# A three-block network on one core: a linear fed by a layer norm's result before the next norm's root is known, re-divided work on the state-space heads, and weight slabs loaded beside the ring

## The reference

```python
# block 1, mixer, state-space part (16 heads of 64, 2 groups)
seg = exp(where(causal, a_cs[l] - a_cs[s], -inf))        # per head, 512 x 512, lower triangle
att = (C @ B.T) * seg
y   = att @ (x * dt)
...
# end of block 1 and start of block 2
x = layer_norm(ALPHA * x + conv_glu_ffn(x), ln3_g, ln3_b)
h = rms_norm(x, norm_mix_2)            # x / sqrt(mean(x^2) + eps) * norm_mix_2
proj = h @ w_in_2                      # first piece: w2_ax, then w2_ac, w2_ab, w2_rx, ...
...
# end of block 2: product-key experts, 8 heads x 16 rows of the expert table per token
q = rms_norm(x, norm_ffn_2) @ w_q_2
rows = expert_table[top16(q @ keys)]   # 512 tokens x 128 rows x 8 KB
y = sum(gelu(rows_u @ h) * gate * rows_v)
```

## Time and profile before

| | before |
|---|---|
| time, median of 3 runs | 3936.34 us (3932.47 to 3937.8) |
| the profiled execution: its own time | 3933.06 us |
| the profiled execution: its span | 3931.0 us |
| mean granted TensorE clock, share of full speed | 0.991 |
| PE busy | 3580.0 us, 91% |
| DVE busy | 2293.1 us, 58% |
| ACT busy | 1487.3 us, 38% |
| POOL busy | 1248.4 us, 32% |
| moved by DMA | 790.33 MB, 201 GB/s over the span |

### The profile page before, as it was taken

One profiled execution on the slowest core, in us unless ns is written; L12 is line 12 of the kernel. 1 busy time (PEld: TensorE's weight loads), 2 busy tenths in 40 slices (PEclk: granted clock), 3 DMA queues, 4 the chain that ended last, 5 costly groups with the idle time before them and its releaser, 6 DMA issues. The chain is left out here.

```text
span 3931.0 us, 39053 instructions
## 1 busy us (share of the span) xinstructions
PE 3580.0 (91%) x14166; PEld 2375.6 (60%) x14166; DVE 2293.1 (58%) x4220; ACT 1487.3 (38%) x3070; POOL 1248.4 (32%) x842
## 2 busy tenths in 40 slices
PE   9989998999999999999777777778779999999999
PEld 7856686788778778643232232232338667678887
DVE  4774533666746374577776777777752863364161
ACT  1233343543232453244444444445443554333222
POOL 0012352454410014233333333333332222244443
PEclk9999999999999999999999999999999999999999
DMA  3211231225622222699999999999972111122222
GB/s 125 91 58 61 68 127 52 77 97 197 256 74 98 89 88 96 268 421 421 418 409 421 421 406 422 421 401 421 421 326 96 54 60 65 57 94 87 96 97 86
DMA packets 113675, 790.33 MB, mean 201 GB/s; under 512 B 13072, under 2 KB 13264, under 8 KB 21840
## 3 DMA queue, kind: packets, MB, share of 16 engines
q0 software_dynamic: 73728, 536.90, 33.0%
q1 hardware_dynamic: 39760, 250.97, 17.9%
HBM read 785.73 MB, written 2.10 MB: 200 GB/s over the span
## 5 line engine op out<-in xcount | busy, mean ns | idle before, releaser
L3134 PE MATMUL bank<-arena 128*128 128x512 f32 x1984 | 965.3, 614 | 244.3 <-ACT arena L3189 222.8
L3134 PEld LDWEIGHTS bank<-arena 128*128 128x128 f32 x1984 | 348.9, 191 | 826.1 <-issue 805.4
L3237 DVE SCALAR_TENSOR_TENSOR arena<-arena,bank 128x1024 f32<-128x1024 f32 x512 | 624.6, 1220 | 345.6 <-DMA arena<-in_experts,arena 341.2
L999 PE MATMUL bank<-rounded,weights_hi 128*128 128x512 f32 (+1 forms) x2056 | 795.1, 387 | 24.0 <-DVE rounded L1099 7.4
L938 POOL TENSOR_TENSOR weights_lo<-weight_ring,weights_hi 128x1024 fp32r<-128x1024 f32 (+3 forms) x219 | 512.0, 2339 | 935.8 <-ACT weights_hi L1027 935.6
L1000 PE MATMUL bank<-rounded,weights_hi 128*128 128x512 f32 (+1 forms) x2056 | 791.7, 385 | 0.0
L1001 PE MATMUL bank<-rounded,weights_lo 128*128 128x512 f32 (+1 forms) x2056 | 791.6, 385 | 0.0
L3224 POOL DMA_INDIRECT arena<-in_experts,arena x512 | 481.5, 940 | 851.7 <-PE bank L3134 712.3
L1027 ACT ACTIVATE weights_hi<-weight_ring 128x1024 fp32r<-128x1024 f32 (+3 forms) x271 | 270.1, 997 | 707.9 <-PE bank L1001 705.7
L999 PEld LDWEIGHTS bank<-rounded,weights_hi 128*128 128x128 f32 x2056 | 386.9, 188 | 110.4 <-issue 22.1
L1001 PEld LDWEIGHTS bank<-rounded,weights_lo 128*128 128x128 f32 x2056 | 387.0, 188 | 77.2
(11 more groups left out here) (467 smaller groups left out, 4530.0 us busy)
## 6 DMA issues: line engine op xcount, KB each, us to landing
arena<-in_w_ada SPq DMA_DIRECT2D x48, 512.0 KB, 8.2
weight_ring<-in_w_up SPq DMA_DIRECT2D x22, 1024.0 KB
weight_ring<-in_w_down SPq DMA_DIRECT2D x8, 1408.0 KB
weight_ring<-in_w_ga SPq DMA_DIRECT2D x8, 1024.0 KB
weight_ring<-in_w_gb SPq DMA_DIRECT2D x8, 1024.0 KB
weight_ring<-in_w_q SPq DMA_DIRECT2D x8, 1024.0 KB
arena<-in_experts,arena POOLq DMA_INDIRECT x512
weight_ring<-in_w_mlp1a SPq DMA_DIRECT2D x8, 1024.0 KB
```

The lines of the kernel that those rows point to most:

```text
L999: pe.matmul(out, hi[:, k - k0, :], x.hi(k), start=first, stop=False)
L3134: mm = pe.matmul(total[:, half * T:(half + 1) * T], diag[:, j, :], rows[:, j, D + half * T:D + (half + 1) * T], start=i % SLOTS == 0, stop ...
L3237: dve.scalar_tensor_tensor(row, row, 1.0, tokens(i // SLOTS), ALU.mult, ALU.mult, accum_out=dots[:, i:i + 1]).then_inc(s.dotted.sem, 1)
```

## The change

Three places are rewritten.

1. **State-space heads.** The cumulative sums are put as two rounded parts (`acs_parts`, 48 rows, with zeros between) and spread by one rounded matmul with a chooser of two ones. DVE's differences cover only the first 128 tokens of each segment; ACT takes the exponential of the rest straight from the bank with the negated column as bias (three instructions) and of the clipped parts in two more. The weighing is divided: DVE the first segment (512), POOL the other three (768). `sums` waits for `exp_ready` of the head four before, no longer for `diff_ready`, and `heads` for POOL too.
2. **The seam.** `w2_ax` takes the layer norm's result times the next norm's weights (`WithoutRoot`: the split halves come from x * gain, without the root). Squares, their sum and the root are made while `w2_ax` runs (`RootBeside`), and `w2_ax` is taken by DVE with a multiplication by the spread inverse root (`take_scaled`). `s.n` and `s.n_split` are made during `w2_ax` for the linears behind it. Of the last group of `modulate`, 4 rows are folded ahead of the taking of the last `w_down` tile, 2 remain in `w2_ax`.
3. **Slabs.** Slabs 2, 3 and 4 of `w2_q` go to free places of the arena (`aside`) as soon as the block begins; the ring takes slabs 5, 6, 7 and those of `w3_nq`.

```diff
-        pe.matmul(self.sum_bank(h), s.eye[0:SSD_HEADS, h:h + 1].broadcast_to([SSD_HEADS, P]), self.acs, start=True, stop=True).then_inc(self.bc_ready.sem, 1)
+        pe.matmul(self.sum_bank(h), self.choose[:, h:h + 1].broadcast_to([3 * SSD_HEADS, P]), self.acs_parts, start=True, stop=True).then_inc(self.bc_ready.sem, 1)
...
     def exp(self, act, h):
+
+        att = self.att[h % 4]
         act.wait_ge(self.diff_ready.sem, self.diff_ready.at(h + 1))
-        act.activation(self.att[h % 4], self.att[h % 4], ACT.Exp).then_inc(self.exp_ready.sem, 1)
...
+        for a in range(TT - 1):
+            act.activation(att[:, SEG[a] + P:SEG[a] + seg_width(a)], self.sum_bank(h)[:, (a + 1) * P:T], ACT.Exp, bias=self.minus_acs[:, a, h:h + 1])
...
+    def weigh_first(self, dve, h):
+        self.weigh(dve, h, (0,), self.att_ready)
+
+    def weigh_others(self, pool, h):
...
+        self.weigh(pool, h, (1, 2, 3), self.others_ready)
...
+    def on_act(self, act, first_weights):
+        x, y = self.first, self.later
...
+        for k in range(DT):
+            self.high(act, k)
+            x.shift(act, k)
+            yield
...
+    def add_made(self, dve, t):
+        for k in {2: (0, 1), 3: (2, 3), 4: (4, 5), 5: (6, 7), 6: ()}.get(t, ()):
+            self.first.scale(dve, k)
+        for k in {3: (0, 1), 4: (2, 3), 5: (4, 5), 6: (6, 7)}.get(t, ()):
+            self.low(dve, k)
...
+    def sum_up(self, pe, t):
+        x = self.first
+        if t == 1:
+            pe.wait_ge(x.used.sem, x.used.at(DT - 1))
+            x.columns(pe, self.total, True, True).then_inc(x.used.sem, 1)
+
+    def midway(self, pe, t):
+        if t == 3:
+            self.first.spreads(pe)
...
+        sync.wait_ge(s.units_done.sem, unit0)
+        for j in aside:
+            sync.wait_ge(*landed(j - RING))
+            sync.dma_start(place(j), s.I["w2_q"][j]).then_inc(landed(j)[0], 16)
```

More of the change, by code:

```diff
@@ L824, in _ @@
         def _(pool):
+            other = beside.pool(pool) if beside.pool else iter(())
             for n in range(ahead, count):
@@ L828, in _ @@
                 pool.tensor_tensor(lo, raw(n), hi.bitcast(F32), ALU.subtract).then_inc(s.lo_made.sem, 1)
+                next(other, None)
             next_low(pool)
+            for _ in other:
+                pass
     if fresh:
@@ L1417, in on_dve, with __init__, high, low @@
             self.low(dve, DT - 1)
+class WithoutRoot(Seam):
+    def __init__(self, s, behind, norm, later, gain_shift, shift_ready, squares):
+        Seam.__init__(self, s, behind, norm)
+        self.later, self.gain_shift, self.shift_ready, self.squares = later, gain_shift, shift_ready, squares
+    def high(self, act, k):
+        x = self.first
+        act.wait_ge(x.scaled.sem, x.scaled.at(k + 1))
+        act.activation(self.split.hi(k), x.dst[:, k, :], ACT.Identity, bias=self.gain_shift[:, k:k + 1], scale=self.later.gain[:, k:k + 1]).then_inc(self.s.act_hi.sem, 1)
+    def low(self, dve, k):
+        x = self.first
+        dve.wait_ge(self.s.act_hi.sem, self.s.act_hi.at(self.round0 + k + 1))
+        dve.wait_ge(x.kept.sem, x.kept.at(k + 1))
+        dve.scalar_tensor_tensor(self.split.lo(k), x.dst[:, k, :], self.later.gain[:, k:k + 1], self.split.hi(k).bitcast(F32), ALU.mult, ALU.subtract).then_inc(self.s.act_lo.sem, 1)
+    def on_act(self, act, first_weights):
+        x, y = self.first, self.later
+        x.ready_for_root(act)
+        yield
+        for t in range(DT):
+            x.square(act, t, (x.centred, x.centred.at(t + 1)))
+            yield
+        x.take_root(act)
+        yield
+        first_weights()
+        act.wait_ge(self.shift_ready.sem, self.shift_ready.at(1))
+        for k in range(DT):
+            self.high(act, k)
+            x.shift(act, k)
+            yield
+        for k in range(DT):
+            act.wait_ge(x.kept.sem, x.kept.at(k + 1))
+            act.activation(self.squares[:, k, :], x.dst[:, k, :], ACT.Square).then_inc(y.squared.sem, 1)
+            yield
+    def add_squares(self, dve):
+        y, total = self.later, self.squares[:, 0, :]
+        for k in range(1, DT):
+            dve.wait_ge(y.squared.sem, y.squared.at(k + 1))
+            if k >= 2:
+                dve.wait_ge(y.used.sem, y.used.at(k - 1))
+            dve.tensor_tensor(total, total, self.squares[:, k, :], ALU.add).then_inc(y.used.sem, 1)
@@ new lines, with __init__, square_made, midway @@
+class RootBeside(Seam):
+    def __init__(self, s, behind, norm, total):
+        Seam.__init__(self, s, behind, norm)
+        self.total = total
+    def add_made(self, dve, t):
[3 more added lines that the diff above has]
+            self.low(dve, k)
+    def square_made(self, act, t):
+        if t == 2:
+            self.first.take_root(act)
+        for k in {3: (0, 1), 4: (2, 3), 5: (4, 5), 6: (6, 7)}.get(t, ()):
+            self.high(act, k)
+    def sum_up(self, pe, t):
+        x = self.first
+        if t == 1:
+            pe.wait_ge(x.used.sem, x.used.at(DT - 1))
+            x.columns(pe, self.total, True, True).then_inc(x.used.sem, 1)
+    def midway(self, pe, t):
+        if t == 3:
+            self.first.spreads(pe)
+    def on_pe(self, pe):
+        yield
+    def on_act(self, act, first_weights):
+        yield
+    def on_dve(self, dve):
+        pass
@@ L1813, in steps_on_dve, with part_rows @@
         dve.tensor_tensor_scan(self.acs, w, d, 0.0, ALU.mult, ALU.add).then_inc(s.rows_done.sem, 1)
+    def part_rows(self, dve, step):
+        s, (high, low) = self.s, (self.acs_parts[k:k + SSD_HEADS, :] for k in (0, 2 * SSD_HEADS))
+        n = 3 * SSD_HEADS
+        dve.tensor_tensor(self.choose, s.eye[0:n, 0:SSD_HEADS], s.eye[0:n, 2 * SSD_HEADS:n], ALU.add)
+        dve.wait_ge(s.rows_done.sem, s.rows_done.at(1))
+        step(dve.tensor_copy(high, self.acs))
+        dve.tensor_tensor(low, self.acs, high.bitcast(F32), ALU.subtract).then_inc(self.cols_ready.sem, 1)
     def turn_rows(self, pe):
```

116 lines of the change are left out of this document (85 added, 31 removed).

## The result

The changed kernel takes 3908.84 us (median of 4 executions, 3907.36 to 3913.55), the kernel before 3937.07 beside it (3932.47 to 3941.18). The ratio is 0.9936, with a 95% interval of 0.9923 to 0.995: faster by 0.5 to 0.8%, where 3906 and 0.8% were predicted. The changed kernel again, later and in five executions, gave 3911.59 against 3935.38, a ratio of 0.9941 (0.9929 to 0.9954). One execution of experiment 6 took 5056 us at a granted clock of 0.761: its median of six counts it, its ratio leaves it out.

The account below looks back on a forecast made before the run. It took DVE to bound the heads, a pure chain the seam and DMA the experts; 11 + 12 + 7.5 = 30.5 us less than 3936.3 gave 3906 us, 0.8% faster, with 8 in 10 between 3896 and 3919.

Parts of the forecast that it names:

- Slabs, -7.5 forecast: Experts' start: three slabs loaded into idle DMA ahead of the first gather save 2.5 us each; from -3 to -8.
- Slabs 5 and 6 now fill just that time: Experts, 1635 to 1700: slabs still loaded while PE is always busy; if DMA runs dry, part of 7.5 us is lost.
- Seam, -12 forecast: Layer norm to `w2_ax`: first matmul 14.5 us earlier, 2.3 us added on PE inside `w2_ax`; from -8 to -13.5.
- up to 1: Ahead of the last `w_down` taking: four foldings are hidden, but two held up by POOL cost up to 1 us.
- PE still runs at its own pace: Inside `w2_ax`: an input tile costs ACT 1.38 us and PE 1.38 us, so PE is not slowed.
- the rival's waits, for `s.n` or at tile 0: Seam: DVE is late and PE waits; -6 us in place of -12, 3912 us; chance 0.12.
- Heads, -11 forecast: State-space heads: period per pair falls from 6.84 to 5.2 us, 11.5 less over seven; from 0 to -17.
- I give back 1.5: Heads: low halves between POOL's weighings and DVE's added row steps, with the first pair about 1 us earlier, cost 1.5 us.
- the products take turns: Heads: POOL's and DVE's weighings do not overlap, 2 x (1.8 + 0.65) = 4.9 us a pair.
- The rival built on it (POOL always first, 8.0 a pair): Heads: DVE's product waits out POOL's for each head, next differences behind it; +8 us on the heads, 3925 us; chance 0.07.
- PE did not pace the heads as a whole: Rival that PE, at 4.4 us a pair, bounds the heads: period near 4.5, heads -16, 3901 us; chance 0.15.
- Single file: Heads: next pair's differences wait for everything of the pair ahead, 9.8 us a pair; 3937.5 us; chance 0.03.

Follow-up runs that it names:

- experiment 6: Changed kernel with the next block's two w_nq slabs loaded only when the last gather has landed; 3910.24 us, ratio 0.9936 to the kernel before.
- experiment 5: Changed kernel with five slabs of w2_q beside the ring instead of three, slabs 5 and 6 in the empty weight halves; 3903.19 us, ratio 0.9917.
- experiment 2: Changed kernel with the whole weighing, all 1280 columns, on DVE and none on POOL; 3906.05 us, ratio 0.9927 to the kernel before.
- experiment 3: Changed kernel with segments 0 and 1 (896 columns) weighed by DVE and 384 columns by POOL; 3906.79 us, ratio 0.9928 to the kernel before.
- experiment 4: Changed kernel with POOL's weighing of each head waiting for DVE's of the same head; 3917.54 us in a single execution.

## Why the prediction was right, and where a term was off

**What bounds each place** was read rightly. Three stages, one behind the other, each with its own limit: each part taken away gives back its own stage and touches no other (of the experts' 6.7 us, 5.7).

**Slabs, -7.5 forecast, 6.7 measured** (5.9 between the gathers; the other 0.9 is not theirs, as the result shows). "Slabs 5 and 6 now fill just that time" came true. What is missing lies in part just where the prediction feared for DMA, in these windows of the changed kernel:

```profile
1640.00:1650.00 10.00, 10.00 (x27) 4.63 (x26) 8.85 (x25) 2.44 (x9) 3.76 (x4) 1.00 1.01 398
1650.00:1660.00 10.00, 10.00 (x25) 4.37 (x24) 9.24 (x26) 4.65 (x16) 4.62 (x5) 1.00 1.00 396
```

At 398 and 396 GB/s for 421, 1.1 us is lost. But DMA's share stays at 1.01 and 1.00, so these rows don't show it idle, and whether it waited for PE there stays open. The next two slabs of experiment 5 were worth their full 2.5 us each.

**Seam, -12 forecast, 9.7 measured.** Its foldings cost 0.5 us, as "up to 1" allowed: 1064.73 less the 8.39 us that the program was early at this point is 1056.34, and the tile is taken at 1056.83. The first matmul came 13.4 us ahead, not 14.5, since the first scaling was 0.75 late and the chain from it to the matmul took 3.27 and not 2.9. The column sums with their wait (0.54 + 0.91) and the spread (0.81, to the next matmul at 1097.39) make 2.26 inside `w2_ax`, the 2.3 of the sum. The step that was wrong is "PE still runs at its own pace". From the first matmul to the 49th, that is over eight input tiles, it was 1107.75 - 1096.74 = 11.01 before and is 1086.68 - 1074.96 = 11.72 now. I had set ACT's 1.38 us a tile beside PE's 1.38 and called it even; ACT's two operations with the hand-over from DVE in each second tile need 1.49. That is 0.7 us. None of the rival's waits, for `s.n` or at tile 0, came. That leaves 13.4 - 2.3 - 0.7 = 10.4 for the measured 9.7. The issues of SP place 0.3 of the rest: what the seam has won is 10.0 us at `w2_ab` (1164.69 - 8.39 - 1146.30), still 9.9 at `w2_o` and 9.65 at `w2_q`. The other 0.4 I can't place.

**Heads, -11 forecast, 8.7 measured.** The period away from disturbances was forecast at 5.2 and is 5.35, and POOL's 1.8 us for 768 columns is 1.82. The mis-sized term is "I give back 1.5" for what stands between weighings. Three of seven periods are 6.6 to 6.9, which costs (6.84 - 5.35) + (6.63 - 5.35) + (6.91 - 5.35) = 4.3 us; the first `heads` comes 1.4 us earlier in its stage, where the prediction had about 1.

- In the first and the sixth period, 3.0 us together, POOL has a low half (234.48 and 264.13). It holds up POOL's own next weighing, and in the first period DVE's product too. I counted it once.
- In the fifth, 1.3 us, the loss is ACT's: a high half of weights and a tile of `w_z`, 1.45 us in a row, push back the exponentials that both weighings wait for. The prediction priced ACT at 3.2 to 3.9 us a pair without these two, so this term stood at nothing.

How the 0.5 us by which two periods are too long in experiment 2, and the 0.9 in experiment 3, divide between ACT and POOL was not tried.

Deeper lies a mistake that the sum hid. I took "the products take turns" from the earlier trace rows and found 4.9 us a pair, but did not work out the same pair *without* POOL. With the durations of the earlier trace rows that is 2 x (1.5 + 4 x 0.34) + 0.7 = 6.4, which would have spoken for dividing. But successive instructions of DVE overlap: four differences take 1.04 from start to start and not 1.37, a product 1.40 and not 1.50, so it is 5.5. The gain of dividing was thus 0.2 us a pair and not 1.2, too little to pay for the long periods.

The rule of the Trainium skill that the prediction set against the change (SBUF — State Buffer, "SBUF: two separate sides": the shared port pair is an exclusive lock and the loser is blocked for the whole instruction) is borne out here in the collisions given above: DVE's product ends 0.55 us behind POOL's end whether it waited 0.7 or 2.1 us, and 0.94 for 896 columns. DVE's takings with one input in a bank (L2038, 0.73 us, as at 242.35 amid the weighing of 242.25) run on beside POOL's weighings. By the same section of the Trainium skill such an operation does not take the shared pair, and the trace agrees. The rival built on it (POOL always first, 8.0 a pair) failed for another reason: DVE fills the time with its differences. The same lock at a smaller scale, with POOL's low halves in the queue, is where a part of the missing 2 us lies.

**The rivals.** PE did not pace the heads as a whole: even at 384 columns the period is 5.05 and not 4.4. It comes near, though. In one period PE does three steps of `w_z` and not two, and has no wait ahead of the next `heads`: 5.36 us in the changed kernel (252.32 to 257.68), 5.22 with 384 columns (249.03 to 254.25). Single file came only when I forced it (experiment 4), and then at 6.6 us, not 9.8.

**The sum.** 30.5 us forecast, 25.1 by stages, every term too large by 0.8 to 2.3 us and none too small. That the time came within 3 us of 3906 is partly luck: the medians fell by 28.2 us, 3.1 more than the changed stages account for, and that is no more than the scatter between executions.

## What to carry to other kernels

Before work is divided between DVE and POOL, write down both versions by distances of starts: what DVE needs alone, and what the sum of both engines' products with two inputs in SBUF needs in turns. Here 768 of 1280 columns on POOL lost 3 us to none, and 384 were level with none within 0.6. Count with them what ACT and POOL do for the weights in between. In a stage that DMA bounds, look for the idle time ahead of it; each 1 MB moved there was worth 1.9 to 2.5 us, until two such savings together no longer added up. And when terms are a few us in 3900, compare stages between fixed marks in the traces, not spans.

## What the runs showed that was not expected

The scatter between executions lies in PE's clock. In the changed kernel PE waits 3.05 and 2.02 us ahead of two `heads`, and the windows behind these waits have a granted clock of 0.69 and 0.66, that is partly the 1.2 GHz level, partly 2.4:

```profile
235.00:240.00 5.00, 5.00 (x21) 2.47 (x18) 3.18 (x5) 1.43 (x5) 5.00 (x3) 0.69 0.44 133
265.00:270.00 5.00, 5.00 (x21) 2.84 (x18) 1.47 (x5) 0.69 (x3) 5.00 (x3) 0.66 0.00 0
```

The `heads` at these places take 4.07 and 3.46 us instead of 2.37. In the trace without slabs, whose code is the same up to there, with the same waits of 3.04 and 2.04, both take 2.38. The two stages that no version changed take 735.9 to 742.3 us and 992.9 to 999.3, over fourteen traces: 6 us of chance in each, as much as a whole term of this change. For the first of them, the shortest (the kernel without the heads part) and the longest (experiment 6):

```profile
288.20:1024.11 735.91, 703.75 (x3160) 542.90 (x3161) 406.35 (x510) 279.88 (x413) 296.06 (x117) 1.00 0.32 113
279.81:1022.07 742.26, 710.03 (x3160) 546.33 (x3161) 404.89 (x510) 280.09 (x413) 296.12 (x117) 0.99 0.31 112
```

PE is busy 6.3 us longer for the same 3160 instructions, at a granted clock of 0.99 for 1.00, and that is the whole difference; DVE, ACT and POOL are busy for the same time within 1.5 us.
